# A hybrid decoder step on one core: the linear-attention stage with tokens on output partitions, the compressed prompt branch on array parts, both scans in a row, and the modulation folded into the norm's gain

## What is computed

```python
u = x * (1 + sc1) + sh1                       # x = LN(input); sc, sh, ga come from silu(c) @ w_ada (adaLN)
z = u @ w_in                                  # 22 tiles of 128 columns and a narrow one
# GLA: 4 heads, key width 64, value width 128, chunkwise with a decayed state
S, o = lax.scan(step, s0, (qs, ks, vs, gs))   # o_inter = (q exp(b)) S ;  o = o_inter + att v ;  S = exp(b_last) S + k^T v
o_g = o_g * rsqrt(mean(o_g * o_g) + 1e-6) * gla_norm_g * silu(r_g)
# NSA: 8 heads in 2 groups; three branches, mixed by sigmoid gates
h = sum(proj[m][:, m:m + nc]) + (pe_bias + b1)        # compress_blocks: blocks of 32 tokens, stride 16
kc, vc = gelu(h) @ w2
o_n = g0 * softmax(q kc) vc + g1 * selected_blocks + g2 * sliding_window
x = LN(ALPHA * x + ga1 * (concat(o_g, o_n) @ w_o))
x = LN(ALPHA * x + ga2 * SwiGLU(x * (1 + sc2) + sh2))
```

## Time and profile before

| | us |
|---|---|
| median of 3 runs (1359.06 to 1361.33) | 1359.13 |
| profiled execution | 1358.04 |
| its span | 1356.3 |
| TensorE busy | 1268.5 (94%) |
| VectorE busy | 681.8 (50%) |
| ScalarE busy | 433.7 (32%) |
| GpSimd busy | 89.3 (7%) |

### The profile page before, as it was taken

How to read it: one execution, slowest core, us unless ns; L and a number is a source line. 1 busy time by engine, 2 the same in 40 slices (tenths; PEclk the granted TensorE clock), 3 DMA queues, 4 the chain that set the end, 5 groups by cost and what they waited for, 6 DMA issues and landing times.

```text
span 1356.3 us, 21135 instructions
## 1 busy us (share of the span) xinstructions
PE 1268.5 (94%) x7779; PEld 997.5 (74%) x7779; DVE 681.8 (50%) x1673; ACT 433.7 (32%) x1039; POOL 89.3 (7%) x162
## 2 busy tenths in 40 slices
PE   7999999787998999999999999599999999999995
PEld 4677776673676787778777878378888888788883
DVE  4733423857775656665666552745545545110013
ACT  4000005124666656755675530411111111000003
POOL 4200000011442000000000000100000000000000
PEclk9899997676998999999999999899999999999997
DMA  9534321413003553465343512411222221112201
GB/s 356 212 126 180 130 99 48 162 31 124 2 1 153 236 216 127 186 263 214 127 186 139 206 70 83 156 58 66 94 77 78 93 68 68 64 65 67 82 21 66
DMA packets 21268, 162.63 MB, mean 120 GB/s; under 512 B 2728, under 2 KB 6920, under 8 KB 11032
## 3 DMA queue, kind: packets, MB, share of 16 engines
q1 hardware_dynamic: 18328, 92.42, 18.8%
q0 software_dynamic: 2736, 69.36, 12.3%
q10 hardware_dynamic: 144, 0.04, 0.0%
HBM read 156.73 MB, written 9.24 MB: 122 GB/s over the span
## 4 chain that ended last, share of the span: by engine, by line
PE 86%; DVE 6%; ACT 4%; issue 3%; DMA 0%; POOL 0%; ACTq 0%; DVEq 0%; POOLq 0%
PE PS L313 79%; PE PS L900 4%; PE PS L1074 3%; ACT sreg L1232 1%; DVE ringreg L1788 1%; PE PS L994 1%; ACT zreg L1385 1%; DVE zreg L1898 0%; PE PS L743 0%; DVE creg L1730 0%; ACT zreg L1375 0%; DVE mixreg L1527 0%; ACT trunk L1237 0%; ACT ringreg L1354 0%; DVE zreg L1926 0%
## 5 line engine op out<-in xcount | busy, mean ns | idle before, releaser
L313 PE MATMUL PS<-zreg,ringreg 128*128 128x272 f32 (+1 forms) x736 | 170.4, 394 | 1.9 <-DVE zreg L2086 1.9
L313 PEld LDWEIGHTS PS<-zreg,ringreg 128*128 128x128 f32 x736 | 141.7, 198 | 30.6 <-issue 2.3
L313 PE MATMUL PS<-creg,ringreg 128*128 128x272 f32 (+2 forms) x576 | 149.6, 414 | 12.1 <-issue 8.8
L313 PE MATMUL PS<-zreg,w 128*128 128x256 f32 (+2 forms) x544 | 140.9, 390 | 4.8 <-DVE zreg L1926 2.9
L313 PE MATMUL PS<-mixreg,w 128*128 128x272 f32 (+1 forms) x596 | 135.8, 379 | 6.6 <-DVE mixreg L1723 6.6
L313 PEld LDWEIGHTS PS<-creg,ringreg 128*128 128x128 f32 (+2 forms) x576 | 106.1, 189 | 43.7 <-issue 18.7
L313 PEld LDWEIGHTS PS<-mixreg,w 128*128 128x128 f32 x596 | 107.8, 190 | 27.7 <-DVE mixreg L1723 7.0
L313 PE MATMUL PS<-mixreg,ringreg 128*128 128x272 f32 x520 | 125.0, 393 | 0.5 <-DVE mixreg L1891 0.5
L313 PEld LDWEIGHTS PS<-mixreg,ringreg 128*128 128x128 f32 x520 | 98.6, 190 | 20.8 <-DVE mixreg L1891 0.6
L313 PE MATMUL PS<-zreg 128*128 128x256 f32 (+4 forms) x320 | 105.2, 411 | 5.0 <-DVE ringreg L1800 1.8
L313 PEld LDWEIGHTS PS<-zreg,w 128*128 128x128 f32 (+1 forms) x544 | 90.9, 189 | 22.3 <-issue 5.2
(11 more groups left out here) (340 smaller groups left out, 1759.1 us busy)
## 6 DMA issues: line engine op xcount, KB each, us to landing
ringreg<-in_w_ada_dram SPq DMA_DIRECT2D x24, 1024.0 KB, 6.4
ringreg<-in_w_f_dram SPq DMA_DIRECT2D x22, 1024.0 KB, 4.8
ringreg<-in_w_in_dram SPq DMA_DIRECT2D x11, 1024.0 KB, 4.9
ringreg<-in_w_f_dram SPq DMA_DIRECT2D x16, 704.0 KB, 4.0
sreg<-in_win_dram SPq DMA_DIRECT2D x8, 512.0 KB
ringreg<-in_w_o_dram SPq DMA_DIRECT2D x4, 1024.0 KB, 7.7
out_dram<-in_win_dram SPq DMA_DIRECT2D x1, 4064.0 KB
trunk<-in_x_t_dram SPq DMA_DIRECT2D x4, 544.0 KB, 5.5
```

Source lines behind the costliest of these rows:

```text
L313: return nc.tensor.matmul(o, lhsT, rhs, start=start, stop=stop, **kw)
```

## The change

Four things are changed. (1) Norm and modulation: the norm's gain and shift are multiplied into scale and shift of the modulation (`fold_gain`), so that `U` is written straight from the normalised tile; ScalarE writes the even tiles and VectorE the odd ones at the start, ScalarE all eight at the feed-forward; gain and alpha for the residual are applied later in one operation (`residual`). The adaLN copies stand between the normalised tiles, the feed-forward's first product uses other PSUM banks and no longer waits for `TW`. (2) Compressed prompt branch: the bias is two extra columns of the compression product; that product is cut in three portions and put between other TensorE work; scores, values and probabilities of the four query groups lie on four 32-partition parts. (3) Linear attention: the prompt output has tokens on partitions (16 tiles of 128 x 128 and one for the samples), so that mean squares are sums along the free axis; the result is scaled, transposed back and multiplied with the gate. The copies of the compressed keys and values stand inside the first scan; the second scan follows at once. (4) GpSimd takes the spread sample values (`VMB`), the gate product (`TH`) and `QBS`, the sample queries spread over batches.

The core of the diff, in the order of the file (`values_of_batches` spreads `VMB` on GpSimd; `ON` holds the 17 output tiles with tokens on partitions, `OSQ` their squares, `gms` their mean squares):

```diff
+                for a_ in range(2):
+                    pool.wait_ge(sem("ln_h"), nth * KD + QT * (a_ + 1))
+                    nc.gpsimd.tensor_tensor(us[:, a_], xs[:, a_], ms[:, chunk + 1, a_].unsqueeze(3).to_broadcast(shp), ALU.mult).then_inc(sem("u_s"), 1)
...
+                if n == 2:
+                    pool.wait_ge(sem("mod_one"), 3)
+                    sample_u(0, 0, 2)
...
+            pool.wait_ge(sem("gla_ket"), 1)
+            nc.gpsimd.memset(QBS, 0.0).then_inc(sem("gla_vm"), 1)
...
+                    nc.gpsimd.tensor_tensor(VMB[2 * hp + lo], VT[0:LS, TT, h * DV:(h + 1) * DV].unsqueeze(1).to_broadcast([LS, DB, DV]),
...
+            pool.wait_ge(sem("cmpp_mm"), 2)
+            values_of_batches(0)
+            pool.wait_ge(sem("gla_th"), 1)
+            nc.gpsimd.tensor_scalar(TH, TH, 1.0, None, ALU.add).then_inc(sem("gla_tm"), 1)
...
+            nc.gpsimd.tensor_tensor(TH, TH, Z[:, ZRG:ZRG + GH, :], ALU.mult).then_inc(sem("gla_tm"), 1)
+            values_of_batches(1)
...
+            def compress_prompt(tiles):
...
+                pe.wait_ge(sem("xtp"), 14)
...
+                        last = matmul(PS[:, cmpp_bank[c], 0:96], W1[:, c, m, j, :], RM[:, 4 * NT + 96 * u + m:4 * NT + 96 * (u + 1) + m],
...
+                if t == 2:
+                    compress_prompt(range(4))
...
-                    last = matmul(PS[0:1, 7, c * HID:(c + 1) * HID], pe_t[:, c, n // JP, n % JP:n % JP + 1], W1[:, c, n // JP, n % JP, :],
...
+            compress_prompt(range(4, 10))
...
+            compress_prompt(range(10, 16))
...
+                    last = matmul(PS[r * NCP:(r + 1) * NCP, 3, P + g * HD:P + (g + 1) * HD], HG[:, 1, g, :], w2[:, 1, :], True, True)
...
+                    last = matmul(PS[r * NCP:(r + 1) * NCP, 6 + g, :], kcTp[g * HD:(g + 1) * HD, :], Z[g * HD:(g + 1) * HD, ZQN + r, 0:LP], True, True)
...
+            def prompt_rows(h):
...
+                    matmul(PS[:, bank, o:o + P], ATT[:, h, t, :], VT[:, t, h * DV:(h + 1) * DV], t % 2 == 0, False, skip_group_check=True)
...
+                        last = matmul(PS[c * CH:(c + 1) * CH, bank, o:o + P], E[2][lo:lo + DK, hp, t * P + c * CH:t * P + (c + 1) * CH],
+                                      SST[hp][lo:lo + DK, t * 4 + c, :], False, True, skip_group_check=True)
...
+            prompt_rows(0)
...
+            pe.wait_ge(sem("nsa_cte"), G)
...
+                    last = nc.tensor.transpose(PS[:, 6 + g, j * P:(j + 1) * P], PCT[:, g, j * P:(j + 1) * P], ident[:, :])
...
+                    last = matmul(PS[h * LS:(h + 1) * LS, 2, 0:P], QBS[:, h // 2, h % 2, b, :], S0[:, h // 2, b, :],
...
+            prompt_rows(1)
+            pe.wait_ge(sem("nsa_cx"), 2)
+            state_update(0)
+            prompt_rows(2)
+            prompt_rows(3)
+            pe.wait_ge(sem("gla_sq"), 2)
+            state_update(1)
...
+                    last = nc.tensor.transpose(PS[:, 6 + g, j * P:(j + 1) * P], pc[:, n * P:(n + 1) * P], ident[:, :])
...
+                    last = matmul(PS[g * HD:(g + 1) * HD, cv_bank[r], :], vcp[r * NCP:(r + 1) * NCP, g * HD:(g + 1) * HD],
...
+                    last = nc.tensor.transpose(PS[:, (4, 5, 0, 1)[n], t * P:(t + 1) * P],
...
-            prompt_out(0, 0)
...
-            mean_square(3)
...
+                if 1 <= n <= KD:
+                    residual(0, n - 1)
...
+                nc.scalar.activation(OSQ[:, 4 * n:4 * n + 4, :].rearrange("p n v -> p (n v)"), PS[:, (4, 5, 0, 1)[n], :], ACT.Square
...
+            nc.scalar.activation(gms[:, :], gms[:, :], ACT.Sqrt).then_inc(sem("gla_rstd"), 1)
...
+            ln_act(1)
...
+            modulated(1, 3, range(KD))
...
+                nc.vector.scalar_tensor_tensor(out=cth, in0=mod[:, chunk + 1], scalar=1.0, in1=shift, op0=ALU.add, op1=ALU.mult).then_inc(sem("mod_one"), 1)
+                nc.vector.scalar_tensor_tensor(out=mod[:, chunk + 1], in0=mod[:, chunk + 1], scalar=1.0, in1=gain, op0=ALU.add, op1=ALU.mult
...
+                nc.vector.tensor_tensor(mod[:, chunk], mod[:, chunk], cth, ALU.add).then_inc(sem("mod_one"), 1)
...
+                if k in (1, 4, 6):
+                    ada_row(3 + k // 2 - (k > 1), 3 + k // 2 - (k > 1), 6)
...
-            nc.vector.memset(QB[0:DK, :, 1, :], 0.0)
...
+                dve.wait_ge(sem("gla_exp"), n + 1)
...
+            prompt_bias(0)
...
+            prompt_bias(1)
...
+                    if h == 0 and c == 3:
+                        dve.wait_ge(sem("cmpp_kv"), 1)
+                        nc.vector.tensor_scalar(kcTp, PS[:, 3, 0:NCP], 0.5, None, ALU.mult).then_inc(sem("cmpp_ev"), 1)
...
+            new_states(0)
...
+                    new_states(1)
...
+                nc.vector.tensor_reduce(gms[:, 4 * n:4 * n + 4], OSQ[:, 4 * n:4 * n + 4, :], AX.X, ALU.add).then_inc(sem("gla_msq"), 1)
+            dve.wait_ge(sem("gla_msq"), 5)
...
+            nc.vector.reciprocal(gms[:, :], gms[:, :]).then_inc(sem("gla_rec"), 1)
...
+                nc.vector.tensor_tensor(ON[:, 4 * n:4 * n + 4, :], PS[:, (4, 5, 0, 1)[n], :].rearrange("p (n v) -> p n v", n=4),
...
+                nc.vector.scalar_tensor_tensor(out=MIXT[:, h, 0:LP], in0=PS[:, (4, 5, 0, 1)[n], :], scalar=gng[:, 0:1], in1=TH[:, h, 0:LP],
...
-                nc.vector.reciprocal(SQG[:, h, :], SQG[:, h, :]).then_inc(sem("gla_rec"), 1)
...
+            dve.sem_inc(sem("blk_sum"), 14)
...
+                    dve.wait_ge(sem("ln_u"), KD // 2 + QT * (n + 1))
+                    dve.wait_ge(sem("u_s"), 14 + 2 * n)
```

More of the change, by code:

```diff
@@ L730, in _ @@
                 last.then_inc(sem("decay_x"), 1)
+            def compress_prompt(tiles):
+                pe.wait_ge(sem("xtp"), 14)
+                pe.wait_ge(sem("w1_in"), 16)
+                for u in tiles:
+                    c, j = u // JP, u % JP
+                    for m in range(2):
+                        last = matmul(PS[:, cmpp_bank[c], 0:96], W1[:, c, m, j, :], RM[:, 4 * NT + 96 * u + m:4 * NT + 96 * (u + 1) + m],
+                                      j == 0 and m == 0, j == JP - 1 and m == 1)
+                    if j == JP - 1:
+                        last.then_inc(sem("cmpp_mm"), 1)
             src = [ZVG + i for i in range(4)] + [ZKV + i for i in range(6)]
@@ L1243, in _ @@
             act.wait_ge(sem("consts_in"), 144)
-            ln_act(0, 0)
+            ln_act(0)
+            act.wait_ge(sem("mod_one"), 3)
+            modulated(0, 0, range(0, KD, 2))
             for n in range(NPAIR):
@@ L1487, in gate @@
                     nc.scalar.activation(FT[k % 2][:, HALF:NT], g2, ACT.Tanh, scale=0.5).then_inc(sem("ff_th"), 1)
+                    if isinstance(i, int) and i == 0:
+                        if k == 0:
+                            act.wait_ge(sem("u_s"), 16)
+                        for x in (2 * k, 2 * k + 1):
+                            residual(1, x)
             full = N_F1 // RING
@@ L1492, in _ @@
             gate(full, N_F1 - full * RING)
-            ln_act(2, 4)
+            ln_act(2)
+            for k in range(KD):
+                act.wait_ge(sem("ln_h"), 2 * KD + k + 1)
+                nc.scalar.activation(X[:, k, :], XC[:, k, :], ACT.Identity, bias=lnv[:, 5, k:k + 1], scale=lnv[:, 4, k:k + 1]).then_inc(sem("ln_x"), 1)
         @block.vector
```

452 lines of the change are left out of this document (210 added, 242 removed).

## The result

| us | before | after |
|---|---|---|
| median, runs taken together (4 each) | 1360.23 (1359.06 to 1361.56) | 1302.82 (1302.12 to 1303.87) |
| profiled execution / span | 1358.04 / 1356.3 | 1303.87 / 1302.1 |

The account below looks back on a forecast made before the run. The chain was taken as 86% TensorE, with lost time in the start, linear-attention stage and feed-forward head. Savings of 3.3 + 43.5 + 9.5 = 56.3 us from the median 1359.13 gave 1302.8, range 1294 to 1317.

Parts of the forecast that it names:

- Start: Before the input projection: earlier row copies, folded gain and split tiles save 3.3 us, between 1.6 and 4.5.
- held by the two sums as before: Start of the input projection: the first pair's later products still wait for two sums over modulated tiles; no size given.
- Rival 4: Start and feed-forward head: weights' landing and sums set the products as before, only the stage gains; 1315 us, chance 0.09.
- Up to the first scan: Linear-attention stage: bias in spare columns lets the first scan start at 243, minus 8.5 us, at worst minus 5.8.
- Scans: Linear-attention stage: the second scan follows the first at once, ending at 255.8 instead of 267.86, 3.6 us more gained.
- Tail: Second scan to next stage's first score product: VectorE's chain of 23.9 us plus 2 for hops, score product at 284.
- The 1.3 us between scan and chain: Tail's beginning: TensorE's scores, head 0 and transposes end at 257.1, after the second scan's end at 255.8.
- The slack behind the chain: Tail: GpSimd's four copies of swapped queries, needed before the score product, are done at 278.1, leaving 5 us.
- Head: Feed-forward's head: earlier release and ScalarE's modulation start the first product 9.5 us earlier, between 8 and 10.
- Rival 1: Linear-attention tail: TensorE stays at half clock, everything behind the last state update moves by 9 us; 1312, chance 0.18.
- Rival 2: Linear-attention tail: GpSimd becomes the bound; at twice the price the end moves 17 us, 1320; chance 0.13.
- Rival 3: Linear-attention stage: small array tiles don't run at once, 118 us instead of 15; about 1406, slower; chance 0.04.

Follow-up runs that it names:

- the first experiment: Changed kernel, but GpSimd's first two products of spread sample values wait for VectorE's small operations on the compressed hidden values; median 1300.67 us, ratio 0.9566.
- the late release: Changed kernel, but the feed-forward's first product is released only behind the four sums of modulated tiles; median 1309.90 us, ratio 0.9631.

## Why the prediction was right, and where not

- **Start: wrong.** Forecast 3.3 us less, measured 0.3 more. (Its terms, 3.3 and 1.7 less and 0.5 to 1.2 more, add up to 3.8 to 4.5, not to 3.3.) Up to the modulated tiles it came as said: they end at 41.42 instead of 44.65, 3.2 earlier. The last row gave 2.5 instead of 3.3, as TensorE waits 1.7 us for weights at 30.4; folding cost 0.9, within its 0.5 to 1.2, as one of its operations is held beside GpSimd's sum (1.20 us, 0.23 without it); the tiles gave 1.6. The step that failed is the last, from the tiles to the stream, "held by the two sums as before". The two sums took 2.24 us each beside GpSimd's instead of 1.29. And the first product's halves, which the prediction left off the path, took 3.97 and 3.96 instead of 3.53 and 2.07: the clock, back in time in before, was so in only four of seven executions. That an earlier product can run at half clock should have been one of this step's bounds. Rival 4 has the start's outcome, but the weights' landing, which it names, is worth only 0.8 of it; at the head it falls.
- **Up to the first scan: 3.2 us late** (246.24 instead of 243; 2.9 counted from the first sum product). Exponentials (232.8, forecast 234) and products (236.1, forecast 236.8) came as said. Nearly the whole miss is GpSimd's hold on the two small operations, 3.0 us by the first experiment. The prediction had the row for it, 1.65 against 1.19, took it for a slowdown of two-operand passes, and asked only about the scans, which are free of it as forecast.
- **Scans: right.** In a row, 12.4 us (forecast 12.8); the gap between them fell from 4.1 to 0.03 us, and with the copies behind the scan it is 2.6.
- **Tail: right in its sum.** From the second scan's end to the score product, 59.6 us became 25.3, which is 34.3 of the stage's 43.9. VectorE's chain took 25.1 us to the end of the swapped copy (258.67 to 283.77); the forecast had 23.9 and 2 for hops. GpSimd held two of its terms: L1799, as shown, by 1.1 us, and the swapped copy, 1.56 us beside GpSimd's copies where 0.9 was forecast. In before, alone, it took

```profile
326.44 0.87 DVE L1800 COPY ringreg<-zreg 64x512 f32<-64x512 f32 x2 [2.13 <-ACT mixreg L1331]
```

The 1.3 us between scan and chain, for TensorE, did not appear: with the clock back at 256, scores, head and transposes took 5.8 us (252.56 to 258.40) and not 7.4. Nor did the 1 us put in for queueing. That is what made up for the late scan: 283.92, forecast 284. The slack behind the chain was 3 us, not 5: four of GpSimd's copies were done at 280.8, forecast 278.1.
- **Head: right.** 10.2, forecast 9.5; the late release splits it.
- **Rival 1** (half clock in the tail): falls as a whole, full clock from 256 to 273; only from 274 on is it half, where the 16 transposes behind the scaling, part of the chain, take 3.67 us.
- **Rival 2** (GpSimd the bound): falls as it was put; its work ended at 262.47 (forecast 262) and nothing waited for it. It cost time in another way, by holding VectorE's operations.
- **Rival 3** (array parts don't overlap): falls. TensorE's timeline of after, full tiles and four parts in turn:

```profile
260.93 1.16 PE L319 MATMUL PS<-sreg,ringreg 128*128 128x128 f32 x8
262.01 1.08 PE L319 MATMUL PS<-creg 64*32 64x128 f32 x32
263.02 0.64 PE L319 MATMUL PS<-creg,ringreg 32*64 32x512 f32 x1
```

32 passes on parts follow within 1.01 us, 0.032 each, as in the earlier trace rows. A change of tiling in front of them is nearly free too: 8 full passes to the next start take 1.08 us, against 0.92 at 0.115 each (half of the 0.23 at half clock in the earlier trace rows). So it costs some 0.16 us by this estimate, not the 0.4 that the prediction allowed. The Trainium skill's rule, "TensorEngine Tiling (Array Packing)", section "Key Properties", that a change of mode drains TensorE, gives no price; the trace leaves room for a small one only.

- **Sum.** The stage, 43.5 of 56.3, was right to 0.4 us with two opposite errors of 3 us inside: that it met the time so closely is luck. The start's loss of 3.6 against forecast is the rest of the gap between 56.3 and 54.2, less 0.7 from the head and 0.4 and 0.35 elsewhere.

## What to carry to other kernels

Before work goes to GpSimd, lay its queue beside VectorE's and mark what VectorE runs out of SBUF in that time: each such operation, however small, can cost the rest of GpSimd's instruction, so GpSimd belongs beside VectorE's work out of PSUM, and small operations on the chain come first. A product that starts earlier can lose its gain again if it then runs at half clock or opens a new wait: read the granted clock and the wait behind the moved product before you count it. Compare marks of one profile, since two executions of the same start differed by 4.5 us here.

## What the runs showed of the hardware

- Where both worked out of SBUF, VectorE and GpSimd shut each other out for a whole instruction. A TENSOR_SCALAR of 128 elements took 1.86 us instead of 0.23 beside a GpSimd product of 1.89, 0.99 beside a GpSimd copy of 1.03; GpSimd's weight sums took 2.37 instead of 1.27 beside VectorE's. Even a GpSimd memset did it to copies: two of VectorE's of 32 and 16 elements (L1743, L1744) took 0.72 and 0.63 us in after, until the memset of 1.81 (232.89) was over, and 0.18 and 0.17 in before; a pass with two operands beside the same memset kept its 1.29. Scans and other operations with one operand in PSUM, and reductions, kept their durations. The Trainium skill, "SBUF — State Buffer", section "Who interferes with whom", states this rule: an exclusive lock for the whole instruction, for which copies and tensor_scalar operations can contend, and operations with two SBUF inputs against a GpSimd instruction that reads SBUF, but not reductions. The traces agree in each of these cases. The prediction had weighed only the shorter sentence of the Trainium skill's "GPSIMD Engine Reference", section "Key points", which speaks of contention.
- The granted clock often fell behind a wait. Behind waits of 2.1 to 2.5 us the products at 46.10, 43.18 and 828.31 above ran in part at 0.50 (7.45, 7.42 and 3.76 us instead of 5.7 and, for the last, 2.07); the one at 39.45 had been at 0.50 since 31. Not every wait did it: behind 2.15 us in front of 813.47 in after the clock stayed at 1.00. In three profiles 15 matmuls that compute nothing kept 1.00 from 26 to 43 us, and both halves of the first product took 2.07 us; in the ten profiles without them the clock fell to 0.50 between 29 and 34, and the first half took 3.5 to 4.0 us.
